# Two-block transformer on one core: half of the recurrence's output norm computed in its drain, GpSimd's small work moved, R's sum a slot earlier

## The reference, cut to what matters

```python
def step(S, inp):                       # per token
    r_t, w_t, k_t, v_t, a_t, b_t = inp
    sa = jnp.einsum('bhij,bhj->bhi', S, a_t)
    S = S * w_t[:, :, None, :] + sa[..., None] * b_t[:, :, None, :] + v_t[..., None] * k_t[:, :, None, :]
    y = jnp.einsum('bhij,bhj->bhi', S, r_t)
    return S, y
...
y = _layer_norm(y, gn_g, gn_b, GN_EPS)  # over the 64 channels of a head
bonus = jnp.sum(rh * kh * r_k, axis=-1, keepdims=True) * vh
y = (y + bonus).reshape(Bsz, T, D_B)
return y * jax.nn.silu(gate)
...
o = jnp.concatenate([out_a, out_b], axis=-1) @ w_out
```

## Time and profile before

| | us |
|---|---|
| median of 3 runs | 2588.97 |
| lowest, highest | 2586.21, 2593.63 |
| the profiled execution | 2594.93 |
| its span, first to last instruction | 2592.4 |
| PE busy | 2459.9 (95%) |
| DVE busy | 1489.1 (57%) |
| ACT busy | 1009.9 (39%) |
| POOL busy | 233.7 (9%) |

### The profile page before, as it was taken

The page is one execution under the profiler, slowest core; times in us unless marked ns, Lnnn a source line. Parts: engine busy times, 40 slices in busy tenths (PEclk is TensorE's granted clock), DMA queues, the critical chain, the costliest instruction groups (busy, mean ns, idle before and its releaser), DMA issues. The chain is left out here.

```text
span 2592.4 us, 47833 instructions
## 1 busy us (share of the span) xinstructions
PE 2459.9 (95%) x19281; PEld 2064.1 (80%) x19281; DVE 1489.1 (57%) x2151; ACT 1009.9 (39%) x1785; POOL 233.7 (9%) x226
## 2 busy tenths in 40 slices
PE   9899999999999999989999999999899999788788
PEld 7889999998887856768888888887677777788666
DVE  5855555545775556377555655677353563455366
ACT  6423333234563269343333333447321512233221
POOL 2000000000000035100000000000010000434500
PEclk9899999999999999999999999999899999699979
DMA  6423343347844500332233234784212112001132
GB/s 181 123 82 130 105 138 120 119 164 233 291 142 160 195 5 2 106 114 90 95 104 105 100 100 158 249 282 139 85 62 81 41 57 80 31 4 37 36 118 97
DMA packets 136170, 295.55 MB, mean 114 GB/s; under 512 B 20797, under 2 KB 29278, under 8 KB 134462
## 3 DMA queue, kind: packets, MB, share of 16 engines
q1 hardware_dynamic: 132224, 279.44, 32.8%
q10 hardware_dynamic: 3776, 13.70, 1.5%
HBM read 221.05 MB, written 70.92 MB: 113 GB/s over the span
## 5 line engine op out<-in xcount | busy, mean ns | idle before, releaser
L1644 PE MATMUL f1ps<-f1ring 128*128 128x512 f32 x308 | 120.6, 392 | 3.1 <-DVE f1ring L1453 2.2
L1644 PE MATMUL f0ps<-f0ring 128*128 128x512 f32 x308 | 121.2, 394 | 0.0
L1646 PE MATMUL f0ps<-f0ring 128*128 128x512 f32 x308 | 120.6, 391 | 0.0
L1645 PE MATMUL f0ps<-f0ring 128*128 128x512 f32 x308 | 120.4, 391 | 0.0
L1646 PE MATMUL f1ps<-f1ring 128*128 128x512 f32 x308 | 119.9, 389 | 0.0
L1645 PE MATMUL f1ps<-f1ring 128*128 128x512 f32 x308 | 119.9, 389 | 0.0
L1540 PE MATMUL f0ps<-b1XH,f0highE 128*128 128x264 f32 (+1 forms) x384 | 110.7, 288 | 4.1 <-DVE f0lowE L1297 4.1
L1897 PE MATMUL w_in_b_pr<-b1XH,w_in_b_wH 128*128 128x512 f32 x272 | 110.1, 405 | 3.4 <-DVE w_in_b_wL L1846 3.4
L1542 PE MATMUL f0ps<-b1XH,f0lowE 128*128 128x264 f32 (+1 forms) x384 | 109.3, 285 | 0.0
L1541 PE MATMUL f0ps<-b1XL,f0highE 128*128 128x264 f32 (+1 forms) x384 | 109.1, 284 | 0.0
L1540 PE MATMUL f0ps<-b1XH,Y_rounded 128*128 128x264 f32 (+1 forms) x384 | 108.5, 283 | 0.0
(11 more groups left out here) (573 smaller groups left out, 7479.5 us busy)
## 6 DMA issues: line engine op xcount, KB each, us to landing
f0hidden<-f0tm SPq DMA_DIRECT2D x74, 256.0 KB, 4.9
f1hidden<-f1tm SPq DMA_DIRECT2D x74, 256.0 KB, 2.9
f0ring_plain<-f0hidden SPq DMA_DIRECT2D x55, 256.0 KB, 3.2
f1ring_plain<-f1hidden SPq DMA_DIRECT2D x55, 256.0 KB, 3.2
b1XH_plain<-in_w_down SPq DMA_DIRECT2D x48, 256.0 KB, 4.5
Y<-in_w_ada SPq DMA_DIRECT2D x8, 1536.0 KB, 6.4
Y<-in_w_gate_up SPq DMA_DIRECT2D x44, 256.0 KB, 2.9
Y<-in_w_gate_up SPq DMA_DIRECT2D x22, 512.0 KB, 3.5
```

Source lines behind the costliest of these rows:

```text
L1644: pe.matmul(o, ah, bh, start=fresh, stop=False, skip_group_check=True)
L1645: pe.matmul(o, ah, bl, start=False, stop=False, skip_group_check=True)
L1646: return pe.matmul(o, al, bh, start=False, stop=last, skip_group_check=True)
```

## The change

In the prelude, POOL's three memsets now stand ahead of its first decays, and the wait for the constants with `back`'s product goes to t = 2, behind the last mask. The bonus pieces go to six places in tiles 5 and 6, and two behind the loop. ACT's `squared` moves from slot 2 to slot 3. DVE's R of the first chunk moves from slot 1 (behind a9) to slot 0 (ahead of `at`). In the drain, PE sums the squares of the first 512 tokens in two groups behind slots 2 and 3, ACT takes their root in slot 4 and DVE the reciprocal in slot 5, into tiles that now live through both stages. In the output stage one `turned` and `broadcast` 0 stand ahead of the other half's sums, whose root stands in ACT's piece 1 and whose reciprocal stands ahead of DVE's piece 2; `broadcast` 4 waits for that one.

```diff
@@ recurrence_stage
+        BONUS = [(NT - 3, 3), (NT - 3, 4), (NT - 3, 5), (NT - 2, 2), (NT - 2, 3), (NT - 2, 4)]
@@ POOL
+                pool.memset(ind[:, :, :], 0.0).then_inc(s_blank, 1)
+                pool.memset(back[:, :, :], 0.0).then_inc(s_blank, 1)
+                pool.memset(eps[:, :], HD * 64e-5).then_inc(s_blank, 1)
                 decayed(0)
                 start(0)
                 decayed(1)
-                pool.memset(ind[:, :, :], 0.0).then_inc(s_blank, 1)
-                pool.memset(back[:, :, :], 0.0).then_inc(s_blank, 1)
-                pool.memset(eps[:, :], HD * 64e-5).then_inc(s_blank, 1)
-                pool.wait_ge(s_cols, 112)
-                ps.mark(pool.tensor_tensor(back[:, :, :].rearrange("p f x -> p (f x)"), back[:, :, :].rearrange("p f x -> p (f x)"), grow[:, :], ALU.mult), "back")
                 for t in range(NT):
                     for l in range(2, LV):
                         other(t, l)
                         if l == 2 and t + 2 < NT:
                             decayed(t + 2)
-                        if t >= NT - 2:
-                            bonus(4 * (t - NT + 2) + l - 2)
+                        if (t, l) == (2, LV - 1):
+                            pool.wait_ge(s_cols, 112)
+                            ps.mark(pool.tensor_tensor(back[:, :, :].rearrange("p f x -> p (f x)"), back[:, :, :].rearrange("p f x -> p (f x)"), grow[:, :], ALU.mult), "back")
+                        if (t, l) in BONUS:
+                            bonus(BONUS.index((t, l)))
                     if t + 1 < NT:
                         start(t + 1)
+                for i in range(len(BONUS), 8):
+                    bonus(i)
                 for t in range(NT - 1):
                     gated(t)
@@ ACT
-                        if h == 2 and t >= 2:
+                        if h == 3 and t >= 2:
                             squared(t - 2)
+                        if h == 4 and t == NT:
+                            pv.wait(act, 0, "v1")
+                            ar.mark(act.activation(sd[0:H], inv[0:H, 0, 0, 0:256], ACT.Sqrt, bias=eps[0:H]), "root")
@@ DVE
-                        if h == 1 and t:
+                        if h == 0 and t:
                             received(t - 1, 0)
...
+                        if h == 5 and t == NT:
+                            ar.wait(dve, 0, "root")
+                            dr.mark(dve.reciprocal(rs[0:H], sd[0:H]), "rate")
@@ PE
+                def variance(j):
+                    if j == 0:
+                        pe.wait_ge(s_cols, 112)
+                        dl.wait(pe, NT - 1, f"a{HL - 1}")
+                        asq.wait(pe, 3, "sq")
+                    for c in range(4):
+                        mm = pe.matmul(inv[32 * j:32 * (j + 1), 0, 0, 0:256], ind[:, c], k[:, c, 256 * j:256 * (j + 1)], start=(c == 0), stop=(c == 3))
+                    pv.mark(mm, f"v{j}")
...
+                        if t == NT and h in (2, 3):
+                            variance(h - 2)
@@ output_stage, PE
-                    if i % 4 == 0:
-                        pe.wait_ge(s_rate, i // 4 + 1)
+                    if i == 4:
+                        pe.wait_ge(s_rate, 1)
...
-                for j in range(4):
+                turned(0)
+                broadcast(0)
+                for j in range(2, 4):
                     for c in range(4):
...
-                for t in range(2):
-                    turned(t)
-                for i in range(4):
+                turned(1)
+                for i in range(1, 4):
                     broadcast(i)
@@ DVE
-                for h in range(2):
-                    dve.wait_ge(s_root, h + 1)
-                    dve.reciprocal(rs[64 * h:64 * (h + 1)], sd[64 * h:64 * (h + 1)]).then_inc(s_rate, 1)
                 for i in range(8):
                     c, x = piece(i)
+                    if i == 2:
+                        dve.wait_ge(s_root, 1)
+                        dve.reciprocal(rs[64:P], sd[64:P]).then_inc(s_rate, 1)
@@ ACT
-                for h in range(2):
-                    x = slice(64 * h, 64 * (h + 1))
-                    act.wait_ge(s_var, h + 1)
-                    act.activation(sd[x], pv[x, h, 0:256], ACT.Sqrt, bias=eps[x, 0:1]).then_inc(s_root, 1)
                 for i in range(8):
                     c, x = piece(i)
+                    if i == 1:
+                        act.wait_ge(s_var, 1)
+                        act.activation(sd[64:P], pv[64:P, 0, 0:256], ACT.Sqrt, bias=eps[64:P, 0:1]).then_inc(s_root, 1)
```

More of the change, by code:

```diff
@@ L2840, in recurrence_stage @@
         center = b.sb(ctx, "center", [P, H])
-        gates, gate_out, a_in, out_a, ind, back, grow, cols, eps = norm
+        gates, gate_out, a_in, out_a, ind, back, grow, cols, eps, sd, rs = norm
         bv = later[0][0]
@@ L2875, in recurrence_stage @@
         ps = marks("pool_scaled", ["back"])
+        pv = marks("pe_var", ["v0", "v1"])
+        ar = marks("act_root", ["root"])
+        dr = marks("dve_rate", ["rate"])
         def rows(i):
@@ L3421, in _, with output_stage @@
                             update(t - 1, HL - 1)
-def output_stage(b, PB, bv, a, gates, ind, back, eps):
+def output_stage(b, PB, bv, a, gates, ind, back, eps, sd, rs):
     with b.stage() as ctx:
         y, sq, z = PB[:, 0:4], PB[:, 4:8], PB[:, 12:16]
-        sd = b.sb(ctx, "norm_sd", [P, 256])
-        rs = b.sb(ctx, "norm_rs", [P, 256])
         pv = b.ps(ctx, "norm_var", [P, 2, 512])
@@ L3463, in broadcast @@
                     mm.then_inc(s_back, 1)
-                for j in range(4):
+                turned(0)
+                broadcast(0)
+                for j in range(2, 4):
                     for c in range(4):
-                        mm = pe.matmul(pv[32 * j:32 * (j + 1), j // 2, 0:256], ind[:, c], sq[:, c, 256 * j:256 * (j + 1)], start=(c == 0), stop=(c == 3))
-                    if j % 2:
-                        mm.then_inc(s_var, 1)
-                for t in range(2):
-                    turned(t)
-                for i in range(4):
+                        mm = pe.matmul(pv[32 * j:32 * (j + 1), 0, 0:256], ind[:, c], sq[:, c, 256 * j:256 * (j + 1)], start=(c == 0), stop=(c == 3))
+                mm.then_inc(s_var, 1)
+                turned(1)
+                for i in range(1, 4):
                     broadcast(i)
@@ L3619, in second_block @@
         eps = b.sb(ctx, "gn_eps", [P, 2])
+        sd = b.sb(ctx, "gn_sd", [P, 256])
+        rs = b.sb(ctx, "gn_rs", [P, 256])
         cols = b.sb(ctx, "gn_b", [P, 4])
@@ L3624, in second_block @@
             grow = b.sb(row, "gn_g", [P, DA])
-            recurrence_stage(b, PB, kk, ab, lw, tris, [(bv[:, :, :], bonus_out)], (gates, gate_out, a, out_a, ind, back, grow, cols, eps[:, 0:1]))
+            recurrence_stage(b, PB, kk, ab, lw, tris, [(bv[:, :, :], bonus_out)], (gates, gate_out, a, out_a, ind, back, grow, cols, eps[:, 0:1], sd, rs))
         right = ExitStack()
         b.alloc_x(right, "b3", SEQ, "right")
-        output_stage(b, PB, bv, a, gates, ind, back, eps)
+        output_stage(b, PB, bv, a, gates, ind, back, eps, sd, rs)
     with right:
```

## The result

The median after is 2596.61 us (2592.38 to 2606.97, 20 runs), beside 2588.97 for the kernel before (20 runs): ratio 1.0032, 95% interval 1.0023 to 1.0040, which is 8.3 us more (6.0 to 10.4; the two medians lie 7.6 apart). The forecast was 2597.2, or +8.2. The total came out as forecast; three of its terms did not.

The account below looks back on a forecast made before the run. No single engine bounds the touched stretches; each is a chain over PE, ACT, DVE and POOL. Terms 0.7 + 3.2 + 0.5 + 0.3 + 0.4 + 3.1 make +8.2 us: median 2597.2, range 2586 to 2602.

Parts of the forecast that it names:

- Memsets, +0.7: Prelude: three memsets now stand uncovered between `center` and POOL's first products, where ACT and PE wait; +0.7 us.
- R, +3.2: Loop: R delays `at`, a9 and PE's product by 0.8 in t = 1 to 5; t = 5's share absorbed, +3.2 us.
- rival at 2594.0: Loop: PE's waits for instructions take up R's delays for t = 1 to 4 too, so the 3.2 go; chance 0.22.
- rival at 2587.7: Loop: sa0 waits for R, so its earlier place gains 0.9 us seven times instead of costing 3.2; chance 0.08.
- `back`, +0.5: Loop, t = 2: `back`'s product delays the next tile's `eye`, which then lies beside DVE's S product; +0.5 us, between 0 and 0.6.
- bonus, +0.3: Loop: t = 6 gives 1.0 back, t = 5's new piece delays PE's transposing matmuls by 1.35; +0.3 us, bounds -1.0 and +1.4.
- Drain, +0.4: Drain: R saves 0.2, first variance group costs 0.2 net, gated products beside DVE's last S cost 0.4; bounds 0 and 1.5.
- The collision of S with GpSimd, priced at 0.4: Drain: POOL's gated products end some 2.3 us later, beside DVE's last S product; up to 0.57, taken as 0.4 us.
- Output stage, +3.1: Output stage: broadcast 4 waits for the second reciprocal, so transposes 2 come later; +3.1 us, bounds -4.9 and +4.3.
- rival at 2598.4: Output stage: half clock lasts through broadcast 1 as well, +1.2 us over the forecast; chance 0.10.
- full clock (rival at 2589.2): Output stage: PE is granted the full clock, DVE binds, term -4.9 and sum +0.2 us; chance 0.15.
- "same" and "slower": Whole kernel: chances 0.52 for same and 0.42 for slower, with 0.3% (7.8 us) as the dividing size.

Follow-up runs that it names:

- mended kernel: Changed kernel with R back in slot 1, output-stage and drain sums reordered, memsets ahead of the mask wait, bonus pieces re-placed; ratio 1.0001 to the kernel before.
- R alone: Kernel before with only R of the first chunk moved to slot 0, ahead of the decay and a9; ratio 1.0035, +9.0 us.
- the pair above: Changed kernel with all repairs, transposes inside broadcasts and root ahead of second SA, with R in slot 1 (ratio 0.9983) or slot 0 (1.0013), against the kernel before.
- R put back: Changed kernel with R of the first chunk back in slot 1, behind a9; ratio 1.0027 to the kernel before, +7.0 us.
- the whole GpSimd part: Kernel before with only GpSimd's edits: memsets, the constant's product at t = 2, bonus pieces; ratio 0.9998, -0.5 us.
- stage mended: Changed kernel with output-stage sums reordered, second reciprocal ahead of piece 1, transposes ahead of the broadcast two pieces on; ratio 1.0019 to the kernel before, stage 29.6 us.
- norm alone: Kernel before with only the norm's edits (drain sums, root, reciprocal, squares a slot later, new output stage), without R's move or GpSimd's edits; ratio 1.0035, +9.0 us.
- PE kept busy: Changed kernel with an added unread matmul of 256 columns between the two matmuls of each output-stage broadcast; ratio 1.0058 to the kernel before, stage 40.2 us.
- second execution of after: Changed kernel, unchanged, timed and profiled again; ratio 1.0046 to the kernel before, +11.9 us.

## Why the prediction was right in its total, and where its terms were wrong

- **Memsets, +0.7: right**, 0.6 and 1.0 by the prelude. Ahead of the wait for the masks they cost nothing (28.1 in the mended kernel).
- **R, +3.2: the wrong term.** "R (0.87 us, 0.8 to the start of the next operation) pushes both" left out what the pushed decay meets. The product comes 1.7 later in each of five iterations, 8.5 in all. The Trainium skill, SBUF — State Buffer, section "SBUF: two separate sides", says that a DVE operation with two SBUF inputs and a GpSimd operation that reads SBUF take turns at a shared port for the whole instruction; the decay's 1.46 beside L2981 fits, which ends 0.55 us behind it. The other half of the term, that instruction waits take some up, isn't settled in size. The seven traces with R in slot 0 have loops of 215.8 to 222.4 (mean 219.7), the six with R behind a9 210.8 to 218.4 (mean 214.5; 213.8 without the kernel before, whose first two iterations are some 4.5 us longer, at half clock). By these means 5.2 to 6.0 of 8.5 stay, and the sum of "issue" in PE's timeline falls from a mean of 18.1 to 15.1; the long wait of the earlier trace rows alone goes from 3.8 to 4.5 in the six to 3.1 to 3.8 in the seven, which is the share that the forecast gave it. Loops of a group differ by up to 7.6, so this is a mean and no measurement of the term. Timings say 9.0 for R alone, 5.9 to 7.8 for the pair above, and 1.3 to 4.9 for R put back. The rival at 2594.0, that these waits take up all, is out by R alone (5.7 to 12.4). That sa0 waits for R (the rival at 2587.7) is out by the same run, for which it meant -6 to -3.
- **`back`, +0.5, and bonus, +0.3: right in place.** The S product takes 0.94 (0.42 before), the wait at t = 5 is 1.4 longer, that at t = 6 1.0 shorter. By timing the whole GpSimd part is -0.5 (-3.1 to +2.1); this doesn't separate +1.5 from 0.
- **Drain, +0.4: mis-sized, +2.2.** "Eight matmuls are about 1.0 us at the full clock" took a mean over the earlier trace rows, where two token groups ran side by side for part of the 6.20 us. Alone, one group's matmuls follow each other at 0.216 us, and eight take 1.85 to the next start. The collision of S with GpSimd, priced at 0.4, was real where no sums stood ahead of it (1.42 and 1.38 in two kernels), and absent in the kernel after.
- **Output stage, +3.1: mechanism right, size +4.4.** The steps are those of the forecast: broadcast 4 waits for the reciprocal, transposes 2 come late, 18.9 from there. The sums took 4.9 and not 3.4. The forecast had 16 matmuls of 256 columns at 1.2 GHz, 0.213 each; at half clock those of one group follow each other at 0.427, and only where the two groups meet do four pairs stand side by side. In the stage mended, where the loop order puts the groups side by side throughout, they took 3.56. That is the missing 1.3; in norm alone, with more of the head at the full clock, the whole term was +2.9. Half clock up to broadcast 1, the rival at 2598.4, was not it: broadcast 1 ran at 1.00 (2459.5 to 2462.8).
- **The full clock (rival at 2589.2) is out.** The prediction set a rule of the Trainium skill (TensorE: Matmul & The Clock Gate, "What's actually happening") against this stretch: a busy PE is let up to the full clock. In the kernel after the stretch from broadcast 4 on has 0.50, and with PE kept busy, 95% of 20.4 us by the profile, it stayed at 0.50. Here the measurement decides.

Read from the traces one by one, the terms, in the order of the forecast's sum, make 0.6 + 5.2 + 0.5 + 0.4 + 2.2 + 4.4 = 13.3; the two timings say 8.3 (6.0 to 10.4) and 11.9 (7.8 to 16.0). So the total was met with terms that were some 5 us too small, and something of up to 5 us stands against them: that +8.2 was met by +8.3 is in part luck. GpSimd's edits cost the drain 2.4 when alone, the norm's 2.2, and together 2.2: 1.0 of the 2.4 was the S product beside GpSimd, and the norm's sums push S out of its way. The rest isn't settled: it is no more than one kernel's loop differs between two executions (4.9).

The chances of the forecast for "same" and "slower" don't follow from those of its rivals: by its own list they come out near 0.6 and 0.35, not 0.52 and 0.42.

## What to carry to other kernels

Before an operation is moved ahead of others on DVE, look at what GpSimd runs at the time to which the others are pushed; the pushed operation can cost more than the moved one. A matmul's duration taken from a group that ran beside another one is no price for it alone, and the loop order that puts two column groups side by side shortens such sums (1.06 against 1.91 us for eight records here). When a stage's head is split, write down for each later step which of its inputs now comes last: the reciprocal that was saved at the head came back behind piece 1. And a repair that shortens one engine's path can bring two others together again, as S and GpSimd in the drain.

## What the runs showed of the hardware

The profiled execution before was 6.0 us above its median. Some 4.5 of this is the clock in the first two iterations: the stretches below are at 0.51 and 1.00 (the kernel before, then the second execution of after), and from 2246.3 to 2253.1 the kernel before is at 0.50 again. From the loop's first product to the first `values` (matmuls of slot 5) it is 11.2 us there and 8.8 to 9.0 in eleven of the other traces; the next iteration takes 26.9, and 24.6 to 24.9 in the five others with R behind a9.

```profile
2226.00:2236.20 10.20, 8.82 (x208) 8.22 (x208) 5.03 (x9) 2.90 (x7) 5.53 (x4) 0.51 0.01 2
```

```profile
2226.00:2236.20 10.20, 8.13 (x324) 7.38 (x323) 6.62 (x11) 3.56 (x10) 5.87 (x5) 1.00 0.02 3
```

PE's waits in the loop that the profile prints as "issue" are waits for instructions, as far as the traces can show it. All 303 of them in the fourteen traces' loops stand at counts of PE's recorded instructions whose remainders by 256 lie within 238 to 242. In each trace the longest of them (the one of the earlier trace rows, 3.1 to 4.5 us) ends 1.2 to 1.5 us after a transfer of 16384 bytes of a DMA queue of the kind "instruction" has landed. Which of these places wait, and how long, differs: their sum in the loop is 10.9 to 20.1 us, and its mean is lower where DVE delays PE (15.1 against 18.1).

DVE's S product (two tensors, 0.42 alone) was lengthened to as much as 1.55 us beside a GpSimd product of two tensors, but it stayed at 0.42 to 0.44 in all 20 cases that lay beside a GpSimd operation of a tensor and a scalar alone (the bonus pieces' first half, 1.57 us). The rule of the Trainium skill cited above would have the two take turns there as well; the measurement decides.
